# Gated products in PSUM, one projection copied by ScalarE, a wait per bank, and the last norm's addition one step earlier, in a two-block transformer kernel

## The reference

```python
# first block, per layer (2 layers), after the two attentions y_a and y_b
gate_a = jax.nn.sigmoid(ga + b_gate[l, :D_MODEL])
gate_b = jax.nn.sigmoid(gb + b_gate[l, D_MODEL:])
merged = gate_a * (y_a @ w_proj_a[l]) + gate_b * (y_b @ w_proj_b[l])
x = x + merged @ w_out[l]
h = rms_norm(x, norm_ffn[l])
u = causal_dwconv(h @ w_up[l], conv_w[l], conv_b[l])     # 3 taps along the tokens
val, gat = u[..., :D_FF], u[..., D_FF:]                  # D_FF = 2816 = 22 chunks of 128
x = x + (jax.nn.silu(gat) * val) @ w_down[l]
# second block (1 layer), after attention
hn = rms_norm_2(h, norm2_g[layer])
h = h + (jax.nn.silu(hn @ w_gate[layer]) * (hn @ w_up[layer])) @ w_down[layer]
return rms_norm_2(h, norm_f_g)
```

## Time and profile before

| | |
|---|---|
| median of 3 runs | 2392.25 us (2392.19 to 2394.22) |
| profiled execution, its own time | 2393.93 us |
| its span, first to last instruction | 2392.1 us |
| TensorE busy | 2335.4 us, 98% of the span, 11106 matmuls |
| GpSimd busy | 1589.5 us, 66% |
| VectorE busy | 1242.4 us, 52% |
| ScalarE busy | 614.4 us, 26% |
| TensorE clock granted, mean | 0.997 of full speed |

### The profile page before, as it was taken

The page is one execution under the profiler, slowest core; times in us unless marked ns, Lnnn a source line. Parts: engine busy times, 40 slices in busy tenths (PEclk is TensorE's granted clock), DMA queues, the critical chain, the costliest instruction groups (busy, mean ns, idle before and its releaser), DMA issues.

```text
span 2392.1 us, 34530 instructions
## 1 busy us (share of the span) xinstructions
PE 2335.4 (98%) x11106; PEld 1759.3 (74%) x11106; DVE 1242.4 (52%) x2116; ACT 614.4 (26%) x1349; POOL 1589.5 (66%) x818
## 2 busy tenths in 40 slices
PE   7999999999999999999999999999999999999997
PEld 5665578878888776655788788887787567887886
DVE  5677653366416536775543665165545755440442
ACT  4334620231101233336202311012322753000001
POOL 5564367777777775543687778777766437777775
PEclk9999999999999999999999999999999999999999
DMA  6122022223223222220233223322362002322222
GB/s 204 63 79 99 18 71 89 96 88 95 90 96 96 88 91 69 79 99 19 63 96 97 88 88 97 97 89 96 125 220 97 19 10 88 97 89 96 91 93 88
DMA packets 61586, 212.65 MB, mean 89 GB/s; under 512 B 6344, under 2 KB 6728, under 8 KB 61328
## 3 DMA queue, kind: packets, MB, share of 16 engines
q1 hardware_dynamic: 54368, 194.38, 25.5%
q10 hardware_dynamic: 7088, 16.58, 2.1%
HBM read 208.78 MB, written 10.01 MB: 91 GB/s over the span
## 4 chain that ended last, share of the span: by engine, by line
PE 89%; DVE 3%; ACT 3%; issue 2%; DVEq 2%; DMA 0%; POOL 0%; ACTq 0%; SPq 0%; POOLq 0%
PE out_tile L509 77%; PE turned L655 3%; PE stat L672 2%; ACT sq L1141 1%; PE out_tile L1013 1%; PE out_tile L729 1%; PE out_tile L827 1%; PE out_tile L832 1%; ACT arena L1151 1%; PE out_tile L837 1%; DVEq L1459 1%; PE turned L632 1%; DMA x<-x_t 0%; PE stat L509 0%; PE out_tile L847 0%
## 5 line engine op out<-in xcount | busy, mean ns | idle before, releaser
L509 PE MATMUL out_tile<-arena_r,w_hi 128*128 128x512 f32 x5240 | 1648.2, 395 | 0.0
L509 PEld LDWEIGHTS out_tile<-arena_r,w_hi 128*128 128x128 f32 x5240 | 984.5, 188 | 239.6 <-issue 1.9
L509 PE MATMUL out_tile<-arena_r,w_lo 128*128 128x512 f32 x2620 | 1046.7, 400 | 15.3 <-POOL w_lo L1914 3.6
L1908 POOL TENSOR_TENSOR w_hi<-weight_ring,cst 128x1024 fp32r<-128x1024 f32 (+1 forms) x348 | 659.4, 1895 | 539.4 <-PE out_tile L509 475.4
L1914 POOL TENSOR_TENSOR w_lo<-weight_ring,w_hi 128x1024 fp32r<-128x1024 f32 (+1 forms) x348 | 850.6, 2444 | 26.8
L509 PEld LDWEIGHTS out_tile<-arena_r,w_lo 128*128 128x128 f32 x2620 | 492.1, 188 | 164.9 <-issue 32.4
L1437 DVE TENSOR_TENSOR x<-out_tile,x 128x512 f32<-128x512 f32 x72 | 49.8, 692 | 339.1 <-PE out_tile L509 339.0
L1258 ACT ACTIVATE work<-out_tile,p 128x512 f32<-128x512 f32 x88 | 65.8, 773 | 375.0 <-PE out_tile L509 263.1
L1372 DVE CAST arena_r<-work 128x512 f32 (+2 forms) x84 | 137.0, 1631 | 13.0 <-issue 11.8
L1374 DVE TENSOR_TENSOR arena_r<-work,arena_r 128x512 f32 (+2 forms) x84 | 135.6, 1614 | 13.4 <-issue 12.1
L1698 DVE SCALAR_TENSOR_TENSOR work<-out_tile,p,work 128x511 f32<-128x511 f32 x88 | 65.6, 745 | 136.7 <-ACT work L1258 136.7
(11 more groups left out here) (213 smaller groups left out, 1835.8 us busy)
## 6 DMA issues: line engine op xcount, KB each, us to landing
weight_ring<-stream SPq DMA_DIRECT2D x356, 512.0 KB, 3.5
arena<-bias_rows ACTq DMA_DIRECT2D x4, 2048.0 KB, 12.1
bias_rows<-bias_kept ACTq DMA_DIRECT2D x2, 2556.0 KB, 22.0
bias_rows<-bias_kept SPq DMA_DIRECT2D x1, 2556.0 KB, 14.3
x<-x_t SPq DMA_DIRECT2D x4, 512.0 KB, 9.6
arena<-w ACTq DMA_DIRECT2D x1, 2048.0 KB, 8.4
out_t<-arena SPq DMA_DIRECT2D x8, 256.0 KB, 2.2
cst<-consts SPq DMA_DIRECT2D x1, 576.0 KB, 14.5
```

The costliest lines, as they stand in the source:

```text
L509: ins = pe.matmul(out, l, r, start=start and n == 0, stop=stop and n == 2, **kw)
L1908: pool.tensor_tensor(blocks_of(w_hi[:, s % SPLIT, :], used), blocks_of(ring[:, s, :], used), cols(cst, C_ONE).unsqueeze(1).to_broadcast([P ...
```

## The change

Four edits.

1. The product of value and silu lies in PSUM instead of SBUF: `product(0)` is `stat[0]`, `product(1)` is `turn[0]`. In section A the second tap (L1702) of tiles 0 and 2 writes it there, after a copy of the first two columns, which that tap doesn't cover; in section B the multiplication writes it. The split then reads PSUM.
2. The tile `pb 0` is released by ScalarE, which copies it to `stat[1]`; VectorE multiplies that copy.
3. In the loops of the up stages TensorE waits for the second bank of a pair only ahead of that bank's first matmul; in section B a wait ahead of each half for all VectorE tiles before it is gone.
4. In the last residual the addition of the seventh square stands ahead of the addition of the last tile to `x`.

```diff
@@ plan_first
-        projections, gates = [(("pb", j), "v"), (("pa", j), "v")], [(("gb", j), "a"), (("ga", j), "a")]
+        projections, gates = [(("pb", j), "v" if j else "a"), (("pa", j), "v")], [(("gb", j), "a"), (("ga", j), "a")]
@@ two_blocks_kernel
+        def product(n):
+            return turn[0] if n else stat[0]
@@ tensor, section A, up stages
                         for s in (0, 2):
-                            pe.wait_ge(A.taken["v"], L * A.count["v"] + i * 4 + (v0 + s - 3))
                             for k in range(DC):
                                 for e in range(2):
+                                    if k == 0:
+                                        pe.wait_ge(A.taken["v"], L * A.count["v"] + i * 4 + (v0 + s + e - 4))
                                     w = weight(i, 4)
@@ tensor, section B, up stages
-                pe.wait_ge(B.taken["v"], v0)
...
                         pe.wait_ge(B.taken["a"], i * 2 + (a0 + s // 2 - 1))
-                        pe.wait_ge(B.taken["v"], i * 2 + (v0 + s // 2 - 1))
+                        pe.wait_ge(B.taken["v"], i * 2 + (v0 + s - 3))
                         for k in range(DC):
                             for e in range(2):
+                                if (k, e) == (0, 1):
+                                    pe.wait_ge(B.taken["v"], i * 2 + (v0 + s // 2 - 1))
@@ scalar, merge
                 norm_upper(L * 3 * DC + DC, h_ffn)
+                A.wait_done(act, L, ("pb", 0))
+                act.activation(stat[1][:, :], psum[A.tile_no(("pb", 0)) % 4][:, :], ACT.Copy).then_inc(A.taken["a"], 1)
                 for j in range(DC):
@@ vector, residual
                 for j in range(DC + 1):
+                    early = norm and not raw and j == DC - 1
+                    if early:
+                        add_square(norm[0], norm[1], j - 1)
                     if j < DC:
                         took(dve.tensor_tensor(x[:, j, :], tile(sec, L, key(j))[:, :], x[:, j, :], ALU.add), sec)
                     if raw and j >= 1:
                         raw_lower(raw[0], j - 1, raw[1])
-                    if norm and j >= 1:
+                    if norm and j >= 1 and not early:
                         add_square(norm[0], norm[1], j - 1)
@@ vector, merge
-                    took(dve.tensor_tensor(work[:, 5, :], tile(A, L, ("pb", j))[:, :], work[:, 2 * (j % 2) + 1, :],
-                                           ALU.mult), A)
+                    if j == 0:
+                        dve.tensor_tensor(work[:, 5, :], stat[1][:, :], work[:, 1, :], ALU.mult)
+                    else:
+                        took(dve.tensor_tensor(work[:, 5, :], tile(A, L, ("pb", j))[:, :], work[:, 2 * (j % 2) + 1, :],
+                                               ALU.mult), A)
@@ vector, section A, up stages
-                            t = work[:, 2 * s:2 * s + 1, :]
+                            t = product(s)[:, :].unsqueeze(1)
                             dve.tensor_tensor(t, t, work[:, 4 + s:5 + s, :], ALU.mult)
...
                             dve.drain()
-                            took(dve.scalar_tensor_tensor(out=work[:, s, 2:S], in0=ps[:, 0:S - 2],
+                            t = work[:, s, :]
+                            if s % 2 == 0:
+                                t = product(s // 2)
+                                dve.tensor_copy(t[:, 0:2], work[:, s, 0:2])
+                            took(dve.scalar_tensor_tensor(out=t[:, 2:S], in0=ps[:, 0:S - 2],
                                                           scalar=p1[:, bass.ds(c, 1)], in1=work[:, s, 2:S],
@@ vector, section B, up stages
-                        t = work[:, s - 1:s, :]
-                        took(dve.tensor_tensor(t, psum[(n0 + s) % 4][:, :].unsqueeze(1), t, ALU.mult), B)
+                        t = product(s // 2)[:, :].unsqueeze(1)
+                        took(dve.tensor_tensor(t, psum[(n0 + s) % 4][:, :].unsqueeze(1), work[:, s - 1:s, :], ALU.mult), B)
```

## The result

| | before | after |
|---|---|---|
| median, runs side by side | 2392.22 us (2391.36 to 2394.22, 6 runs) | 2378.15 us (2377.42 to 2379.27, 6 runs) |
| profiled execution, its own time | 2393.93 us | 2378.82 us |
| its span | 2392.1 us | 2377.0 us |

The ratio is 0.9941, 95% interval 0.9928 to 0.9954: 14.1 us (0.59%) faster. The forecast was 10.7 us less, 2381.6 us, with a range of 2379 to 2386.5. So the direction was right, and the gain is larger than the range allowed. The interval stands for 11.0 to 17.2 us, so these few runs alone don't say how much of the surplus is real.

What follows compares the result with a forecast made beforehand. TensorE, busy 98% of the span, was taken as the bound, so only gaps in its matmul row count: 2.7 + 1.2 + 3.5 + 2.5 + 0.75 = 10.7 us off the median 2392.25 gives 2381.6 us, range 2379 to 2386.5.

Steps and rivals of the forecast that it cites:

- The merge: Layers 1 and 2: ScalarE's copy frees the bank of `pb 0` early, closing TensorE's gap before `gb 1`; 2 x 1.36 = 2.7 us.
- the product in PSUM: Section A's second-half down stages: the last hidden chunk's chain shrinks from 5.52 to 2.4 us, closing two gaps; 3.5 us.
- section B's entries: Start of section B's two halves: without the wait for earlier tiles, gaps of 1.05 and 1.42 us close; 2.5 us.
- the last norm: Last residual: the earlier addition lets the root start sooner, held by ScalarE's table load; 0.75 us, at most 0.95.
- its own third term: Products in PSUM, section A's down stages: 3.5 us, though a rule says an undisturbed cast gets slower with a PSUM operand.
- The up entry: First up loop in section A, twice: three matmuls go ahead of the second bank's wait; 2 x (0.70 - 0.10) = 1.2 us.
- The extra waits: One more TensorE wait per pair inside the up loops, 60 in all, taken to cost 0.
- The small copy: Rival, 8 in 100: GpSimd holds up the two-column copies at the up loops' entry; sum 6.3 us, time 2386.0.
- No gap was handed on: Rival, 10 in 100: work behind the removed releasers makes new waits; half back gives 2387 us, two thirds 2388.7.
- The waits broke no row: Rival, 4 in 100: the 60 added waits drain TensorE's queue, 0.24 us or more each; 2396 to 2398 us.
- No edit failed to do its work: Rival, 5 in 100: products stay slow as silu lies in SBUF, 3.5 us lost, one more term fails; about 2388 us.
- I take the sum off the median: Last step, whole kernel: the summed 10.7 us is subtracted from the median, 2392.25 us, giving 2381.6 us.

Runs made afterwards that it cites:

- waits_only: Kernel before with only the per-bank waits, and without the wait ahead of section B's halves: 2386.86 us, ratio 0.9979.
- before_again: The kernel before, unchanged, for a second trace and more timed runs: 2392.42 us, ratio 1.0003, profiled span 2387.1 us.
- last_only: Kernel before with only the seventh square's addition moved ahead of the last tile's: 2390.48 us, ratio 0.9997.
- one_nop: Kernel before with one more VectorE instruction, a semaphore increment, ahead of the last residual before the FFN norm: one run, 2390.86 us.
- waits15: Changed kernel with fifteen waits a pair instead of one in the up loops, 840 satisfied waits added: one run, 2377.84 us.
- no_psum: Changed kernel with the products back in SBUF, the three other edits kept: 2384.53 us, ratio to before 0.9972.
- after_again: The changed kernel, unchanged, for a second trace and more timed runs: 2380.9 us, ratio to before 0.9956.
- after_third: The changed kernel, unchanged, traced and timed a third time: 2377.52 us, ratio to before 0.9944, span 2375.9 us.
- psum_only: Kernel before with only the gated products in PSUM, in both sections: 2387.82 us, ratio 0.9987.

## Why the prediction was right in its parts and wrong in its total

**The merge** (2.7 us forecast; 2.70 measured at the gaps, 2.88 with what follows eight blocks later), **the product in PSUM** (3.5; 3.54), **section B's entries** (2.5; 2.46) and **the last norm** (0.75; 0.76) came out to a few hundredths in the whole change, and to about 0.1 us alone. The method was right: the start that was due, 0.23 us a matmul from the last one, against the start that came, plus 0.10 us for the restart. For the last norm it was right that ScalarE's table load, and not TensorE, is what the root waits for next. In the merge one step was wrong without harm: ScalarE's copy doesn't wait for `pb 0` alone, it stands behind ScalarE's work for the norm and came some 10 us later. What the prediction set against its own third term, that a cast which nothing disturbs gets slower by the edit, came true and didn't matter. The cast in the chain of the earlier trace rows, before:

```profile
813.98 0.43 DVE L1372 CAST arena_r<-work 128x512 f32 x1 [0.18 <-issue]
```

In the changed kernel it takes 0.69 us (the row at 805.82 above), while the multiplication and the subtraction beside it fall from 2.50 and 2.22 us to 0.70 and 0.69.

**The up entry** was mis-sized: 1.2 us forecast, at most 1.4, and 1.52 measured. Of "0.70 - 0.10" the second number was wrong. The two-column copy takes 0.16 us in the row above, but `waits_only`, which hasn't got it, gains the same, and the rest of the difference is a start that follows the tap by 0.05 us (506.65 + 0.75 against 507.45) where it had followed by 0.14 (510.40 + 0.75 against 511.29).

**The extra waits** cost nothing, as taken. **Not forecast**: 0.7 us in the FFN norm, tied to the edit of the merge but not explained, and +0.35 us in section B's attention, which comes with the whole change and isn't explained either. Together the change is worth 11.5 us by the staircase, 11.2 by the two traces without events, and 11.4 by the lowest of 83 runs of before (2388.71 us) and the lowest of 16 of after (2377.36). The sum, 10.7, was short by 0.5 to 0.8 us.

**The rivals.** The small copy wasn't held up by GpSimd: 44 of them took 163 to 165 ns each. The changed kernel's row for the first half of them:

```profile
L1718 DVE COPY stat<-work x22: 163/164/165, 504.9 to 1621.6; 128x2 f32<-128x2 f32 x22
```

(shortest, median and longest in ns.) It goes from SBUF to PSUM; the casts that are held go from SBUF to SBUF. No gap was handed on: at none of the eight places stands a new releaser, and the square in the last norm was in the working. The waits broke no row. No edit failed to do its work.

**The step that failed** is the last one of the sum: "I take the sum off the median". It takes for granted that whatever is in the time of before and isn't touched by an edit stays as it is. The median of before contained events of chance. Over all 83 runs it is 2392.27 us, 3.6 us above the lowest; for after, over 16 runs, it is 2378.49, 1.1 us above the lowest. So of 13.8 us between the pooled medians 11.4 are the edits, and 2.4 come from fewer or rarer events in the median execution. Of the 3.4 us by which 2378.15 lies under the forecast, 0.5 to 0.8 are terms of the sum and the rest is this. How large it is changes from series to series: the medians of the three series of after lie 14.1, 11.0 and 14.8 us under those of before. How often each occurs, from the traces, counting intervals at the lower clock in the latent parts, and from the timed runs, by the mean granted clock on record for each:

| timing between the layers | traces, intervals in each | timed runs at 0.997 or less |
|---|---|---|
| as before (before, before_again, last_only; one_nop: trace alone) | 2, 0, 2, 1 | 50 of 88 |
| shifted (the others; waits15: trace alone) | 1, 1, 1, 1, 1, 1, 1, 0, 0, 0 | 15 of 73 |

In the 77 runs of before with a clock on record, the 43 at 0.997 all took 2392.02 us or more and the 34 at 0.998 or 0.999 all took 2391.72 or less. So the median of before is made by stretches at the lower clock, as far as three places can say. (The mean also takes in the stretch at the lower clock behind the last matmul, 6 us of the first trace.)

Two intervals in one execution are seen only where the timing between the two layers is that of before. `last_only`, whose edit comes after both, kept them. The clocks of the timed runs fit, with one exception: `no_psum` shortens layer 1 too, and 6 of its 8 runs are at 0.997. The other six shifted kernels have 9 of 65. The medians of the single edits are too noisy to add to this. The cause is supported, not settled: that the shift of layer 2 against layer 1 makes the second interval rarer was not shown by itself, and `no_psum` speaks against it. How often GpSimd's split comes before the cast at the start is just as open: the long cast came in traces of both kernels. What such events do to a median of five shows `after_again`: its five runs lie 2.8 to 3.7 us above the lowest of `after_third`, and in its trace a long cast (1.9 us more) and one interval (1.5) make the same sum.

The range was too narrow at its low end for the same reason. It was built from the bounds of the edits alone, while the trace of before held a 1.87 us cast at 26.88 us, where a neighbour four times its size took 0.41, and a window at half the clock with busy engines around it. Both could have been read before the forecast. Nobody could have said whether they would stay; but a range that reached 3.6 us further down would have said that.

## What to carry to other kernels

Cost an edit at the row of the engine that bounds the kernel, at the place: the start that was due against the start that came. That method was good to 0.16 us a place here. Then ask what in the profiled execution isn't the kernel's: an instruction many times longer than its like, a stretch at the lower clock. Such events are worth as much as a small edit, they can come and go with the timing, and where the forecast gain is a half per cent they belong in the range on both sides; the lowest of many runs compare two kernels better than the medians do, but few runs may hold none without an event (the lowest of the 11 of `psum_only` gave 1.5 us for steps of 3.4), and the traces, place by place, do it best. Next to a busy GpSimd, give VectorE's fp32 instructions a PSUM operand where a bank is idle and TensorE waits for the chain: it cut a chain of 5.52 us to 2.45. The cast that nothing held up went from 0.43 to 0.69 us by it, which cost TensorE nothing here.

## What the runs showed that was not expected

- TensorE can fall to 1.2 GHz inside a kernel that keeps it 98% busy, at the end of a group of 32*32 matmuls, in some executions and not in others of the same program; each fall costs 1.5 to 1.6 us.
- A cast of 128x128 from SBUF to SBUF took 0.23 us or 1.87 to 1.95 us at the same place of the same program, the latter where GpSimd's split had begun up to 0.11 us before it.
- 840 satisfied waits ahead of TensorE's weight blocks cost nothing that could be measured.
- An unchanged stretch of VectorE's code paused 0.54 us or 0.19 us depending on an edit elsewhere, in seven traces each; it stays unexplained.
